# Halving the small steps that VectorE slips between its transposes

## The reference, cut to what matters

```python
v1, i1 = lax.top_k(s1, PEER_TOPK)
v2, i2 = lax.top_k(s2, PEER_TOPK)
cand = (v1[..., :, None] + v2[..., None, :]).reshape(ntok, PEER_HEADS, PEER_TOPK * PEER_TOPK)
top, idx = lax.top_k(cand, PEER_TOPK)
e1 = jnp.take_along_axis(i1, idx // PEER_TOPK, axis=-1)
e2 = jnp.take_along_axis(i2, idx % PEER_TOPK, axis=-1)
gates = jax.nn.softmax(top, axis=-1)
act = gelu(einsum('nhkd,nd->nhk', expert_u[experts], tok)) * gates
out = einsum('nhk,nhkd->nd', act, expert_v[experts])
```

## Time and profile before

| what | value |
|---|---|
| median of 3 runs | 2554.84 us (2553.33 to 2555.28) |
| the profiled execution | 2553.92 us, span 2551.8 us |
| TensorE busy | 2500.1 us, 98% of the span |
| VectorE busy | 1818.0 us, 71% |
| ScalarE busy | 1331.8 us, 52% |
| GpSimd busy | 790.2 us, 31% |
| mean granted TensorE clock | 0.998 |
| stage U | about 1053 to 1846 us from the span's start |
| VectorE's steps of picking | 1055.7 to 1312.9 us |

### The profile page before, as it was taken

The page is one execution under the profiler, slowest core; times in us unless marked ns, Lnnn a source line. Parts: engine busy times, 40 slices in busy tenths (PEclk is TensorE's granted clock), DMA queues, the critical chain, the costliest instruction groups (busy, mean ns, idle before and its releaser), DMA issues.

```text
span 2551.8 us, 47449 instructions
## 1 busy us (share of the span) xinstructions
PE 2500.1 (98%) x14050; PEld 2169.4 (85%) x14050; DVE 1818.0 (71%) x3148; ACT 1331.8 (52%) x2526; POOL 790.2 (31%) x604
## 2 busy tenths in 40 slices
PE   8999998999999999999999999999999999999998
PEld 7899997998788878888888888888888888888886
DVE  5567977665766656699987888888766666666666
ACT  5446544234455454444546666666555555555555
POOL 0001104443000000498988888888600000000000
PEclk9999999999999999999999999999999999999999
DMA  6665661001566656655555555555566665666654
GB/s 209 188 191 156 177 195 42 18 26 49 165 192 196 213 163 185 186 182 172 184 177 174 176 162 163 163 162 162 163 192 194 191 196 190 194 193 219 216 192 162
DMA packets 303353, 429.21 MB, mean 168 GB/s; under 512 B 27061, under 2 KB 234407, under 8 KB 302375
## 3 DMA queue, kind: packets, MB, share of 16 engines
q1 hardware_dynamic: 303271, 428.12, 54.5%
HBM read 423.82 MB, written 4.19 MB: 168 GB/s over the span
## 4 chain that ended last, share of the span: by engine, by line
PE 66%; issue 22%; POOL 7%; DVE 3%; ACT 1%; SPq 0%; DMA 0%; POOLq 0%; DVEq 0%; ACTq 0%
PE PS L439 15%; PE PS L865 9%; PE PS L867 9%; PE PS L866 9%; PE PS L441 7%; POOL w_lo L1331 7%; PE PS L431 2%; PE PS L433 2%; PE PS L432 2%; PE PS L829 2%; PE PS L681 1%; PE PS L664 1%; PE PS L624 1%; DVE raw L1863 1%; PE PS L438 0%
## 5 line engine op out<-in xcount | busy, mean ns | idle before, releaser
L439 PE MATMUL PS<-act_both,w_hi 128*128 128x512 f32 x2720 | 963.3, 398 | 10.4 <-POOL w_lo L1331 9.2
L1345 DVE TENSOR_TENSOR w_lo<-raw,w_hi 128x512 fp32r<-128x512 f32 x1064 | 707.6, 691 | 234.0 <-ACT w_hi L893 231.0
L1331 POOL TENSOR_TENSOR w_lo<-raw,w_hi 128x512 fp32r<-128x512 f32 x512 | 665.4, 1313 | 570.8 <-ACT w_hi L1164 551.1
L893 ACT ACTIVATE w_hi<-raw 128x512 fp32r<-128x512 f32 x1064 | 635.9, 624 | 359.0 <-PE PS L487 145.2
L441 PE MATMUL PS<-act_both,w_lo 128*128 128x256 f32 x2550 | 713.1, 280 | 0.0
L439 PEld LDWEIGHTS PS<-act_both,w_hi 128*128 128x128 f32 x2720 | 506.8, 188 | 126.0 <-POOL w_lo L1331 11.9
L441 PEld LDWEIGHTS PS<-act_both,w_lo 128*128 128x128 f32 x2550 | 481.2, 189 | 2.6
L1164 ACT ACTIVATE w_hi<-raw 128x512 fp32r<-128x512 f32 x512 | 316.5, 630 | 239.2 <-PE PS L441 127.0
L865 PE MATMUL PS<-w_hi,act_both 128*128 128x512 f32 x1024 | 398.4, 389 | 1.7 <-DVE w_lo L1345 1.7
L867 PE MATMUL PS<-w_hi,act_both 128*128 128x512 f32 x1024 | 398.4, 389 | 0.0
L866 PE MATMUL PS<-w_lo,act_both 128*128 128x512 f32 x1024 | 398.3, 389 | 0.0
(11 more groups left out here) (273 smaller groups left out, 2681.7 us busy)
## 6 DMA issues: line engine op xcount, KB each, us to landing
raw<-in_peer_u SPq DMA_DIRECT2D x1024, 128.0 KB, 2.7
raw<-in_peer_v SPq DMA_DIRECT2D x256, 512.0 KB, 4.5
raw<-in_w_in SPq DMA_DIRECT2D x180, 512.0 KB, 3.8
raw<-in_w_out SPq DMA_DIRECT2D x32, 512.0 KB, 4.7
raw<-in_peer_w_q SPq DMA_DIRECT2D x128, 128.0 KB, 3.0
raw<-in_w_ret_branch SPq DMA_DIRECT2D x16, 512.0 KB, 4.6
raw<-in_w_rwkv_branch SPq DMA_DIRECT2D x16, 512.0 KB, 4.7
big<-in_x SPq DMA_DIRECT2D x2, 1024.0 KB, 6.1
```

The lines of the kernel that those rows point to most:

```text
L439: last = pe.matmul(PS[:, bank, :], wh, act_both[:, kc, :, :].rearrange("p w n -> p (w n)"), start=start, stop=stop)
L893: act.activation(w_hi[:, slot % 2, hh * 512:(hh + 1) * 512], raw[:, slot, hh * 512:(hh + 1) * 512], ACT.Copy).then_inc(S["unit_hi"], 1)
L1331: pool.tensor_tensor(w_lo[:, k % 2, cols].rearrange("p (c s i) -> p c s i", c=4, s=4), u_part(k, 4 * hh, 4), w_hi[:, k % 2, cols].bitcast( ...
L1345: dve.tensor_tensor(w_lo[:, slot % 2, cols], raw[:, slot, cols], w_hi[:, slot % 2, cols].bitcast(f32), ALU.subtract).then_inc(S["unit_spli ...
```

## The change

A step of `top16` covers half as many rows: 2 rows of 128 or one of 256. There are then 40 steps instead of 20 in each of the four calls of `top16`, 188 in all instead of 108, with as many `link` waits more. The pair steps and the one-hot steps keep their size. `u_turn` takes a function that it calls between the transposes of the two halves. From unit 2 to unit 99 a unit takes two steps, one between its two transposes and one where the step stood before. There was no step between the two transposes of a unit before.

```diff
             def top16(src, n, vout, iout):
 
-                few = n // 4
+                few = n // 8
...
-            def u_turn(it, k):
+            def u_turn(it, k, between=None):
 
                 dve.wait_ge(S[f"raw_in{k}"], it * 64 + (LANDED["u"] + 64))
                 for hh in range(2):
                     turned = u_part(k, 4 * hh, 4)
                     dve.transpose(turned, turned).then_inc(S["uT"], 1)
+                    if between and hh == 0:
+                        between()
...
-            def u_step(unit):
-                u_turn(unit // 4, unit % 4)
+            def u_step(unit, between=None):
+                u_turn(unit // 4, unit % 4, between)
                 if unit >= 4 and unit % 2 == 0:
                     usum(unit // 4 - 1, unit % 4 // 2, False)
             picks = pick_steps()
             for unit in range(4 * PICKED_AT + 4):
-                u_step(unit)
-                if 1 <= unit < 4 * EXP_AT:
+                picking = 2 <= unit < 4 * EXP_AT
+                u_step(unit, (lambda: next(picks, None)) if picking else None)
+                if picking:
                     next(picks, None)
-                    if unit % 4 == 0:
-                        next(picks, None)
```

## The result

The changed kernel takes 2563.91 us (median of 6 runs, 2562.63 to 2566.3), the kernel before beside it 2554.38. The ratio is 1.0038, with a 95% interval of 1.0028 to 1.0048. The forecast was 2559.2 with a range to 2563, most of the chance on no measurable change. The kernel is measurably slower, by more than twice the forecast 4.4 us, and just outside the range.

A forecast was written before the change was run, and what follows sets the result against it. VectorE's late usum in the picking stretch was taken to hold up TensorE. Losses 0 + 8.1 + 7.4 + 1.0 = 16.5, less 12.1 before, made it 4.4 us slower: 2559.2 us, range 2552 to 2563.

The forecast's parts named there:

- What bounds the kernel: Picking stretch: VectorE is nearly full and hands over usum late; stage U loses 12.1 us up to unit 98.
- The slack of 2.5 us: Picking stretch: a usum may be 2.5 us late before TensorE stands still; lateness beyond that is lost for good.
- The mechanism of the change: Two steps a unit: small steps fit in TensorE's 5.66 us per two units, one-hot steps exceed it by 2.33 us.
- Start: Up to unit 28: nothing lost, where 3.5 us were lost before; pair steps of unit 22 leave VectorE 2.0 late.
- First one-hot stretch: Units 43 to 48: usum of unit 50 is 10.6 us late, less 2.5, so 8.1 us lost.
- 4 x 1.24 = 7.99: One-hot stretches: VectorE's work per two units, with transposes and usum, is 7.99 us against TensorE's 5.66.
- is level by unit 64: Behind the first one-hot stretch: VectorE gains 0.7 us per two units in best-8 steps and catches up by unit 64.
- Second one-hot stretch: Units 90 to 95: VectorE ends 9.9 us late in unit 96, less 2.5, so 7.4 us lost.
- End: Steps end in unit 96, not 88, ahead of the exponential before unit 100: 1.0 us more lost, between 0 and 1.5.
- all fit: Small steps: with 80 more steps, 8.0 us more VectorE time, their work per two units stays within TensorE's 5.66 us.
- The rival of the multiplies: One-hot stretches: multiplies hold up GpSimd's subtractions, 4 x 1.0 us more, 2563 us; chance 0.17.
- The rival of the full VectorE: Picking stretch: only the total of VectorE's work counts, 2.5 us faster, 2552.3; decides if slack is 5 us or more; chance 0.13.

The follow-up runs named there:

- e1_behind: Changed kernel with both steps of a unit behind its usum, none between the transposes: 2562.01 us, 1.0027 of the kernel before.
- e2_pace: Changed kernel with large steps only behind the usum at the old pace, 5 in 4 units, small ones 5 in 2 units: 2562.92 us, 1.0032.
- e3_psum: Changed kernel with the one-hot multiply reading its second operand from a copy in PSUM: 2560.48 us, 1.0022 of the kernel before.
- e4_fewwaits: Changed kernel with a top16 step waiting for itself only at the end of a pass, 20 waits instead of 160: 2562.23 us, 1.0028.
- e5_onehot2: Kernel before with only the one-hot steps taken two in a unit, behind the usum, instead of 5 in 4 units: 2561.35 us, 1.0028.
- e6_before_psum: Kernel before with the one-hot multiply's second operand in PSUM: 2554.36 us, 1.0001 of the kernel before.
- e7_pace_fewwaits: e2_pace with a top16 step waiting for itself only at the end of a pass, 20 waits for 160: 2551.05 us, 0.9985.
- e12_before_fewwaits: Kernel before with a top16 step waiting for itself only at the end of a pass, 20 waits instead of 80: 2549.78 us, 0.9985.
- e9_even_waits: Changed kernel's own steps spread evenly by cost, all behind the usum, with the 160 waits and both multiply operands in SBUF: 2556.98 us, 1.0011.
- e11_even_fewwaits: e8_even with both multiply operands in SBUF again (steps spread evenly, few waits): 2545.17 us, 0.9961 of the kernel before.
- e8_even: Changed kernel's half steps spread evenly by cost, all behind the usum, few waits, multiply's second operand in PSUM: 2541.70 us, 0.9953 of before.
- e10_even_between: e8_even with the first step of a unit between its two transposes: 2544.79 us, 0.9962 of the kernel before.

## Why the prediction was wrong

The bookkeeping of the kernels, from the first best-8 step to the transposes of unit 98: the length by the timeline, what VectorE waited for others, and the difference, its work.

| kernel | length us | waited | work | measured, ratio |
|---|---|---|---|---|
| before | 279.3 | 9.5 | 269.8 | 1 |
| changed | 287.7 | 8.4 | 279.3 | 1.0038 |
| e1_behind | 286.3 | 7.6 | 278.7 | 1.0027 |
| e2_pace | 287.7 | 5.8 | 281.9 | 1.0032 |
| e3_psum | 285.8 | 9.3 | 276.5 | 1.0022 |
| e4_fewwaits | 286.1 | 21.0 | 265.1 | 1.0028 |
| e5_onehot2 | 288.0 | 17.6 | 270.4 | 1.0028 |
| e6_before_psum | 279.0 | 9.6 | 269.4 | 1.0001 |
| e7_pace_fewwaits | 275.8 | 11.4 | 264.4 | 0.9985 |
| e12_before_fewwaits | 275.6 | 14.3 | 261.3 | 0.9985 |
| e9_even_waits | 284.5 | 2.4 | 282.1 | 1.0011 |
| e11_even_fewwaits | 271.4 | 7.8 | 263.6 | 0.9961 |
| e8_even | 267.9 | 6.8 | 261.1 | 0.9953 |
| e10_even_between | 271.5 | 10.6 | 260.9 | 0.9962 |

**What bounds the kernel** was read rightly: `usum` behind gelu, copy and subtraction sets TensorE's pace. The slack of 2.5 us held behind the first one-hot stretch: 13.8 less 2.5 against 11.5 read at unit 84 in the changed kernel, 12.7 less 2.5 against 10.3 in e1_behind, 12.2 less 2.5 against 9.8 in e4_fewwaits. It is not the whole rule. Where the clock fell while TensorE had work, TensorE lost more than that: by 1.4 us in e5_onehot2, by 1.9 in the changed kernel at unit 100, and in e9_even_waits, where the latest `usum` before is 15.2 late, unit 90 reads 15.5. In e7_pace_fewwaits it is 0.9 more (10.4 less 2.5 against 8.8 at unit 98) with no fall; that is not explained.

**The mechanism of the change** was right as far as it went: small steps got better, one-hot steps two a unit got worse, and e5_onehot2 makes 7 us of loss with them alone. What failed are terms of the sum, which gave 4.4 and should have given 9.7:

- *Start.* I had nothing lost, it was 0.7. The gain is 2.8, not 3.5. I had unit 22, with the pair steps, 2.0 late; it was 2.9.
- *First one-hot stretch.* I had 8.1, it was 10.8. The step of the prediction was "4 x 1.24 = 7.99" per two units; it was 8.6 (1177.73 to the `usum` of unit 46, two units on). Most of the difference is the multiply, 1.82 from start to start (1180.18 to 1182.00) in place of 1.24: three of them in the stretch took 1.7 to 1.8 us. The transposes are another 0.1: with a step between them one takes 0.64 us (1175.25 to 1175.89), where I had half of a pair, 0.615. (My last sum of the stretch, 7.8 to unit 50, is also 0.2 more than its parts, 7.6.) Unit 50 was 12.9 late against 0.7 at unit 42, 12.2 instead of 10.6. Then "is level by unit 64" was false: unit 68 was at 11.2, 0.8 more than the 10.4 that TensorE had lost by then, and the pair steps of unit 69 came on top. Unit 70 at 13.8 set the loss, 0.9 more than unit 50 had.
- *Second one-hot stretch.* I had 7.4, it was 8.5, with two long multiplies.
- *End.* I had 1.0 more than before, it was 1.8 (3.8 against 2.0), and not by the exponential. 1.9 us were lost in units 96 and 97, with the clock at its lower level, and behind them no more than before: TensorE was late enough for the exponential. In e1_behind and e4_fewwaits, with no such fall, the end is 3.1 and 3.2, 1.1 more than before, which is the step as I had it. So the fall adds some 0.7 net.

Behind the second of these stands a judgement: I put the 80 added waits at 8.0 us of VectorE's work and called them covered, as the small steps "all fit". The work rose by 9.5 us (269.8 to 279.3), of which most is the waits: 0.10 us each by e4_fewwaits (14.2 us for 140), 0.14 by e12_before_fewwaits (8.5 for 60). They are mostly covered in the changed layout, since taking them out wins 2.5 us. They cost far more in the two layouts that space the large steps: 12 us between e2_pace and e7_pace_fewwaits, 12 between e9_even_waits and e11_even_fewwaits (the clock fell in both kernels with the waits and in neither without, so a part of the 12 is the clock's). So the loss has two causes that cover each other. The large steps alone cost 7 us on the kernel before (e5_onehot2). With them spaced but the waits kept, e2_pace wins next to nothing; e9_even_waits wins back 7 us and is still slower than before. With the waits out but the large steps close together 2.5 us are won (e4_fewwaits). With both seen to, the kernels are faster than before (e7_pace_fewwaits, e11_even_fewwaits, e8_even).

**The rival of the multiplies** had the right place and the wrong payer. The Trainium skill's sentence on the shared interfaces (GPSIMD Engine Reference, 1. Specifications) fits: with one operand of the multiply in PSUM its long cases and those of the subtractions beside it are gone. But the price was mostly VectorE's own multiply, 1.2 to 1.77 us, not GpSimd's subtraction: in e3_psum `usum` itself is 2.0 us less late at unit 96. Together it was 2.5 us at most, not 4 on top of my sum.

**The rival of the full VectorE** (2552.3) was not decided by a larger slack. Its condition was not met: VectorE stood still for 8.4 us up to unit 98 in the changed kernel, where the rival reckoned with the 2.6 of before. e9_even_waits comes close to the condition (2.4 us waited) and is slower than before all the same. It has 12.3 us more work than the kernel before up to unit 98, and the 9.5 us that VectorE waits there in the kernel before, most of them behind its last step in unit 88, do not cover that.

What stays open: why the clock fell in some of these kernels and not in others, and so how much of each difference between two kernels is its share. No run changes the clock alone.

## What to carry to other kernels

When small work of one engine is tucked between handovers to others, write down for each stretch its work per handover against the pace of the bound, with the largest step at its real length. Space the large steps rather than cut the small ones (cutting the large ones was not run). What an added wait costs depends on the layout: the same 140 waits were worth 2.5 us where large steps made the loss, and 12 where those were spaced. So do both: take out the waits (in the kernel before 4 us for three lines), spread by cost, and put steps behind what the next engine waits for (3 us in e8_even).

## What the runs showed of the hardware

TensorE's granted clock fell to its lower level, 1.2 GHz, for some 3.4 us three times in the picking stretch of the changed kernel, at about 1190, 1330 and 1347 us; in the picking stretch of the kernel before it never did. The first time, windows and timeline of the changed kernel:

```profile
1189.00:1194.00 5.00, 4.55 (x17) 3.89 (x18) 4.93 (x5) 1.24 (x2) 4.12 (x4) 0.66 0.34 105
```

```profile
1191.74 0.63 PE L439 MATMUL PS<-act_both,w_hi 128*128 128x512 f32 x1
...
1192.38 0.63 PE L439 MATMUL PS<-act_both,w_hi 128*128 128x512 f32 x1
```

A pair of products takes 0.64 us (1191.74 to 1192.38) instead of 0.35. TensorE had stood 1.8 us in front of its product at 1189.45, 2.8 in front of that at 1329.04, before the second fall, and 2.1 in front of that at 1345.72, before the third. Such a wait is not enough for a fall: in e1_behind TensorE waited 2.3 us twice, and its clock did not fall. The first fall cost next to nothing, since TensorE waits for VectorE there anyway: in both kernels the loss of the first stretch is the lateness less 2.5. The third cost 1.8 us: TensorE started unit 96 20.1 us late and was 21.9 late two units on.

A VectorE operation with two SBUF inputs beside GpSimd's subtraction was slowed as well as slowing: 1.18 us alone, up to 1.78 beside it in the changed kernel (five of eight multiplies), up to 2.35 in e11_even_fewwaits, and the pair step 2.2. And a wait of VectorE for its own last instruction costs 0.10 to 0.14 us each time, in this kernel with its instructions of 0.2 to 0.4 us. Instructions that follow without it overlap: in e8_even the one behind the FIND_INDEX8 of 1063.42 us, which lasts 0.28, starts at 1063.62.
